# Small identity products into unread PSUM banks, at twelve places of TensorE's program

## What is computed

```python
for layer in range(2):
    shift, scale, gate = modulation(silu(c), w_mod[layer])      # c_ctx for context tokens
    h = x * (1 + scale) + shift
    if layer == 0:                                             # even
        q, k, v, g, gates = split(h @ w_in)
        y = concat(retention(q, k, v), mlstm(q, k, v, gates)) @ w_out
    else:                                                      # odd
        q, k, v = split(h @ w_in)
        y = concat(gqa(q, k, v), diff_attention(q, k, v)) @ w_out
    x = layer_norm(ALPHA * x + gate * y)
    x = layer_norm(ALPHA * x + gate2 * peer(modulate(x)))       # product keys, top 16, expert rows
```

## Time and profile before

| what | value |
|---|---|
| time, median of three executions | 2671.81 us (2669.43 to 2677.14) |
| the profiled execution's own time | 2669.78 us |
| its span, first to last instruction | 2668.0 us |
| mean granted clock of TensorE | 0.989 |
| PE busy | 2596.5 us (97%), 15833 matmul instructions |
| DVE, ACT, POOL busy | 1658.8 (62%), 1021.3 (38%), 721.4 us (27%) |

### The profile page before, as it was taken

The page is one execution under the profiler, slowest core; times in us unless marked ns, Lnnn a source line. Parts: engine busy times, 40 slices in busy tenths (PEclk is TensorE's granted clock), DMA queues, the critical chain, the costliest instruction groups (busy, mean ns, idle before and its releaser), DMA issues. The chain is left out here.

```text
span 2668.0 us, 39467 instructions
## 1 busy us (share of the span) xinstructions
PE 2596.5 (97%) x15833; PEld 2300.9 (86%) x15833; DVE 1658.8 (62%) x3309; ACT 1021.3 (38%) x1531; POOL 721.4 (27%) x688
## 2 busy tenths in 40 slices
PE   7998999999999999999999989999999999999998
PEld 6997799999999997777779679999999999777775
DVE  3447789888344455555576469987934445655556
ACT  3434433345333333333353553334533333333333
POOL 1001020000111136777712003000011112777773
PEclk9998999999999999999999899999999999999999
DMA  9653474457798869999964624344779886999995
GB/s 308 214 172 139 166 239 138 159 200 296 294 340 312 310 244 389 389 384 380 388 192 147 212 97 154 108 164 168 288 281 360 309 316 223 390 389 391 393 385 202
DMA packets 233941, 708.88 MB, mean 266 GB/s; under 512 B 22432, under 2 KB 154912, under 8 KB 211488
## 3 DMA queue, kind: packets, MB, share of 16 engines
q1 hardware_dynamic: 172912, 516.86, 53.1%
q0 software_dynamic: 60032, 189.01, 19.2%
q10 hardware_dynamic: 816, 0.48, 0.1%
HBM read 602.31 MB, written 103.98 MB: 265 GB/s over the span
## 5 line engine op out<-in xcount | busy, mean ns | idle before, releaser
L1411 PE MATMUL hidden_ps<-h_hi,u_hi 128*128 128x384 f32 x2016 | 680.2, 337 | 4.3 <-issue 3.3
L1411 PE MATMUL hidden_ps<-h_hi,u_lo 128*128 128x384 f32 x2016 | 673.9, 334 | 0.0
L1411 PE MATMUL hidden_ps<-h_lo,u_hi 128*128 128x384 f32 x2016 | 673.9, 334 | 0.0
L2301 DVE TENSOR_TENSOR v_lo<-v_slot,v_hi 128x1024 fp32r<-128x1024 f32 x248 | 303.8, 1225 | 273.1 <-ACT v_hi L2165 273.0
L2165 ACT ACTIVATE v_hi<-v_slot 128x1024 fp32r<-128x1024 f32 x248 | 263.0, 1060 | 514.7 <-PE out_ps L2094 513.0
L2094 PE MATMUL out_ps<-v_hi,act_hi 128*128 128x512 f32 x992 | 389.6, 393 | 0.0
L2094 PE MATMUL out_ps<-v_lo,act_hi 128*128 128x512 f32 x992 | 386.3, 389 | 0.0
L2094 PE MATMUL out_ps<-v_hi,act_lo 128*128 128x512 f32 x992 | 385.9, 389 | 0.0
L1411 PEld LDWEIGHTS hidden_ps<-h_hi,u_hi 128*128 128x128 f32 x2016 | 378.6, 188 | 7.0 <-issue 7.0
L1411 PEld LDWEIGHTS hidden_ps<-h_lo,u_hi 128*128 128x128 f32 x2016 | 378.7, 188 | 0.0
L1411 PEld LDWEIGHTS hidden_ps<-h_hi,u_lo 128*128 128x128 f32 x2016 | 378.5, 188 | 0.0
(11 more groups left out here) (510 smaller groups left out, 3956.1 us busy)
## 6 DMA issues: line engine op xcount, KB each, us to landing
u_slot<-in_peer_u SPq DMA_DIRECT2D x64, 2048.0 KB, 8.9
v_slot<-in_peer_v SPq DMA_DIRECT2D x64, 2048.0 KB, 10.2
hidden<-hidden_ring SPq DMA_DIRECT2D x64, 768.0 KB, 5.8
spread_gates<-spread SPq DMA_DIRECT2D x16, 2048.0 KB, 7.3
hidden_in<-hidden SPq DMA_DIRECT2D x64, 512.0 KB, 14.6
ada_w_ring<-in_ada_w SPq DMA_DIRECT2D x48, 512.0 KB, 5.0
even_w_ring<-in_even_w SPq DMA_DIRECT2D x16, 1024.0 KB, 7.5
ada_w_ring<-in_ada_w SPq DMA_DIRECT2D x16, 1024.0 KB, 6.1
```

Of the source, the lines that this page charges most:

```text
L1411: mm = pe.matmul(PH_[:, b, 0:T], u[:, b, k * P:(k + 1) * P], x[:, k, :], start=(k == 0 and part == 0), stop=(k == KB - 1 and part == 2))
L2301: dve.tensor_tensor(lo, V[o // JC % 2][:, o % JC, :], hi.bitcast(F32), ALU.subtract).then_inc(vl, 1)
```

## The change

The helper becomes `hold_clock(pe, bank, n)`, which issues n such products into the first 128 columns of a bank that is named at each call. It takes no semaphore and signals none. The two calls at the front grow from 6 to 18 and 26, and ten more calls are put in, with 4, 8, 12, 20, 16, 6, 16, 24, 24 and 24 products (in the order of the diff). Two waits are new: in `even_project` on `mix_taken`, and at the end of `odd_project` on `taken`; they make sure that the bank has been read by its real reader.

```diff
--- before.py
+++ after.py
@@ -144,6 +144,11 @@
                     mm = pe.matmul(PR[32 * i:32 * i + 2, m % 2, 0:HALF_COLS], CT[:, 4 * kk + i, :], AW[:, 4 * kk + i, :],
                                    start=(kk == 0), stop=(kk == 1))
             mm.then_inc(used, 1)
+
+        def hold_clock(pe, bank, n):
+
+            for _ in range(n):
+                pe.matmul(bank[:, 0:P], ident, ident, start=True, stop=True, skip_group_check=True)
 
         def cond_slot(k, q):
 
@@ -361,10 +366,6 @@
                             if g == PAIRS - 1:
                                 mm.then_inc(item_done, 1)
 
-                    def keep_warm(n):
-                        for _ in range(n):
-                            pe.matmul(PG[:, 0:P], ident, ident, start=True, stop=True)
-
                     def ret_begin(h):
                         if h:
                             pe.wait_ge(o_taken, h)
@@ -416,13 +417,13 @@
                     pe.transpose(PG[:, 0:2 * DEPTH * 2 * KB], LNR[:, :],
                                  CST[0:2 * DEPTH * 2 * KB, C_IDENT:C_IDENT + 2 * DEPTH * 2 * KB]).then_inc(ln_turned, 1)
                     pe.wait_ge(lnc_done, 1)
-                    keep_warm(6)
+                    hold_clock(pe, PG, 18)
                     pe.wait_ge(xt_taken, KB)
                     first_mod(0)
                     first_mod(1)
                     first_columns(0)
                     first_columns(1)
-                    keep_warm(6)
+                    hold_clock(pe, PG, 26)
                     for g in range(PAIRS):
                         if g + 1 < PAIRS:
                             first_mod(2 * g + 2)
@@ -485,8 +486,11 @@
                                 mm = pe.matmul(PG[:, 6 * R + i * 6:6 * R + (i + 1) * 6], CST[0:R, C_SEL + i * P:C_SEL + (i + 1) * P],
                                                SM[:, :, :].rearrange("p t j -> p (t j)"), start=True, stop=True)
                             mm.then_inc(small_done, 1)
+                    pe.wait_ge(mix_taken, TT)
+                    hold_clock(pe, PG, 4)
                     pe.wait_ge(row_ready, REST // 4)
                     part_columns(pe, PM, ROW, PICK, (REST // 4 - 1) % 2, N_MOD - 1, turned)
+                    hold_clock(pe, PG, 8)
 
                 @block.scalar
                 def _(act):
@@ -1069,6 +1073,7 @@
                         mm.then_inc((f_half, f_done)[n], 1)
                         if (t, n) == (0, 1):
                             turn_mix(2)
+                    hold_clock(pe, PT[:, 0], 12)
                     turn_tile(pe, PF, 1, normed, x_turned)
                     groups = front_groups(PQ, PH_, WQH, UH)
                     pe.wait_ge(first_w, 4)
@@ -1282,6 +1287,7 @@
                             if t == TT - 1 and k == 0:
                                 turn_tile(pe, PF, 0, normed, x_turned)
                         mm.then_inc(f_done, 1)
+                    hold_clock(pe, PT[:, 0], 20)
                     turn_tile(pe, PF, 1, normed, x_turned)
                     groups = front_groups(PQ, PH_, WQH, UH)
                     pe.wait_ge(first_w, 4)
@@ -2490,6 +2496,9 @@
                                     mm = pe.matmul(PJ[:, item % 4, 0:NW], h[:, k, t * P:(t + 1) * P], w[:, k, :],
                                                    start=(k == 0 and part == 0), stop=(k == KB - 1 and part == 2))
                             mm.then_inc(done, 1)
+                    items = NCH * TT - TAKEN
+                    pe.wait_ge(taken, items - 3)
+                    hold_clock(pe, PJ[:, items % 4], 16)
 
                 @block.scalar
                 def _(act):
@@ -2658,6 +2667,7 @@
                         for k, x in enumerate(src):
                             mm = pe.transpose(banks(n)[:, k * P:(k + 1) * P], x, ident)
                         mm.then_inc(turned, 1)
+                    hold_clock(pe, PO[:, 1], 6)
                     for taken in (turn_taken, turn_taken_v):
                         pe.wait_ge(taken, len(TURNS) // 2)
 
@@ -2720,6 +2730,8 @@
                     for n in range(len(GROUPS)):
                         if n + 1 < len(GROUPS):
                             scores(n + 1)
+                        if n == 0:
+                            hold_clock(pe, PO[:, 1], 16)
                         modulation(n)
                         pe.wait_ge(e_done, n + 1)
                         if n >= 1:
@@ -2731,6 +2743,7 @@
                         if n:
                             weighted(n - 1)
                     weighted(len(GROUPS) - 1)
+                    hold_clock(pe, PT[:, 0], 24)
 
                 @block.scalar
                 def _(act):
@@ -2952,6 +2965,8 @@
 
                     def states(h):
                         pe.wait_ge(k_rows, h + 1)
+                        if h == H - 1:
+                            hold_clock(pe, PK, 24)
                         for n, (t, d) in enumerate(KINDS):
                             if h and n % 2 == 0:
                                 pe.wait_ge(cu_taken if n else nc_taken, h)
```

## The result

The changed kernel takes 2681.76 us (median of 8 executions, 2681.05 to 2684.15), the kernel before beside it 2672.84 (8 executions, 2669.4 to 2677.14): ratio 1.0038, 95% interval 1.0028 to 1.0047. It is slower by 8.9 us, clear of noise and above the 8.0 us that the prediction took as the bound; forecast were 2685.2, +15.4 on the profiled run. The profiled execution of the changed kernel took 2681.65 us, with a span of 2679.9.

A forecast was written before the change was run, and what follows sets the result against it. The prediction took TensorE, busy 2596.5 of 2668.0 us, to bound the kernel. Its terms by place summed to +15.4 on the profiled 2669.8, giving 2685.2 us, with a range from 2670 to 2696.

The forecast's parts named there:

- The price: At every hold: one call, two instructions, costs 0.255 us, so 186 more calls add 47.4 us of PE work.
- rival 3: All holds: a long run of calls is cheaper than six, at 0.18 us a call; sum +0.9, 2671, no change; chance 0.10.
- Before the mLSTM: 4 and 8 calls at the joint: start +1.8 us later, 2.5 gained from the clock behind; −0.7.
- Last states: 24 calls in the mLSTM ahead of four products: DVE's copy goes from 241.02 to 245.1; +4.1 us.
- mLSTM's end: 24 calls at the mLSTM's end: +4.2 us of delay, 2.7 gained in the low stretch behind; +1.5.
- Even output block: 12 calls, 3.06 us, in a pause of 1.85; no low stretch behind, so nothing comes back; +1.2 us.
- Into attend: Calls of 16, 6 and 16: delays 3.6, 0.6 and 2.0 us, 4.7 back where exponentials set the pace; +1.5.
- Odd output block: 20 calls, 5.10 us, ahead of eight transpositions; the low stretch lies ahead of the hold; next_ht waits longer; +5.1 us.
- Front: 18 and 26 calls at the kernel's start: the better clock is gained and given away; +1.1 us.
- Rival 1: All holds: they don't keep the clock up, so the gains go; 26.5 us later, about 2696, slower; chance 0.09.
- rival 2: Delays are absorbed later, since what follows a block waits for HBM weights; sum 6.7, 2676, no change; chance 0.15.
- rival 4: All holds: loads of a repeated operand cost nothing, 0.12 us a call; sum −8.2, 2662, faster; chance 0.08.

The follow-up runs named there:

- e2: The changed kernel without the 24 calls ahead of the mLSTM's last states: 2677.17 us, ratio 1.0028 to the kernel before.
- e6: The kernel before with only the 16 calls in attend's first group added (the two new waits stay in): ratio 0.9993 to the kernel before.
- e1: The changed kernel without the 20 calls in the odd output block: 2677.76 us, ratio 1.0034 to the kernel before.
- e3: The changed kernel with the two calls at the front at 6 and 6 as in the kernel before: 2682.68 us, ratio 1.0049 to the kernel before.
- e11: The changed kernel with 40 calls for 20 in the odd output block: 2685.48 us, ratio 1.0046 to the kernel before.
- e12: The changed kernel itself, measured and profiled again without any edit: 2682.65 us, ratio 1.0038 to the kernel before.
- e10: The kernel before plus calls at last states (24), even output block (12), odd projection's end (16), odd output block (20) alone: 2683.14 us, ratio 1.0041.
- e7: The change with all counts cut to the pauses, and without the 4 and 8 calls in attend: ratio 0.9968 to the kernel before.
- e5: The changed kernel without calls at the last states, even output block, odd projection's end and odd output block: 2675.96 us, ratio 1.0011 to the kernel before.
- e9: The change with all counts cut to the pauses, and without the 6 calls in the even output block: 2665.74 us, ratio 0.9972 to the kernel before.

## Why the prediction was right, and where it was not

The side and the mechanism were right: the holds keep the clock up, their overhang costs more than they give, and it is handed on. The size was not: +15.4 worked out, +8.9 measured, within the range given. That 2681.76 lies only 3.4 from the 2685.2 is partly luck: the sum was laid on an execution of 2669.78, and the median of before beside the change is 2672.84. By its own steps:

- **The price.** 0.255 us was the row of six calls; runs of 18 to 40 cost 0.223 to 0.234. The prediction's own sums are +15.4 at 0.255 and +0.9 at 0.18, so about +10.6 at 0.23: the price makes some 4.8 of the 6.5 us that were too many. Six, 18, 26 and 40 calls took 1.53, 4.21, 5.98 and 8.93 us; by these a call is some 0.22 and a run some 0.2 more, once (an estimate), which weighs most on the row of six. It was rival 3 in part. The Trainium skill's pair ("TensorE: Matmul & The Clock Gate", Back-to-back issue gap), 81 ns, stays below the 0.1115 to 0.117 that an instruction took here.
- **Before the mLSTM**, −0.7: the joint cost 1.4 (4.67 − 3.24) for 1.8, and 3.1 came back for 2.5 (26.75 − 23.66 in e2). −1.7. That is against the draw of the clock in before; e6, without calls there, has a shorter stretch and 24.81, against which only 1.2 came back.
- **Last states**, +4.1: 3.5 in e1, e3, e11 and e12, and 5.0 in the first profile, where the hold ran partly at half clock (5.1 in e10). So of the seven stretches this one stayed, in part, and the last, which the prediction left low, was high. Against its block's start DVE's last copy was 1.9 and 0.4 later in the two profiles of the change, not 4, since the better clock ahead of it gave back; in e10, without the joint's calls, 5.1.
- **mLSTM's end**, +1.5: 3.2 of delay (4.2 forecast), 2.7 of gain as forecast (1.5 against e6 and e10, whose stretch there is shorter: 34.33). +0.5.
- **Even output block**, +1.2: 0.7 of delay. That nothing is behind it was wrong: it keeps out a stretch that costs 5.3 to 5.4 us where it falls. The step "no low stretch is behind it" read one execution as a rule.
- **Into attend**, +1.5: 2.9 and 1.9 of delay, against 3.6 and 2.6, and 4.6 of gain in the walk (4.7 forecast). +0.2. ACT did set the pace: PE waits on exp_t in the walk after.
- **End of attend**, +1.6: 2.0 of delay and 1.1 of gain. +0.9.
- **Odd output block**, +5.1: 4.4. That its stretch at 1587 would stay was wrong for both profiles of the change, e2 and e3, and right for e1, e7, e10 and e11. Against its block's start next_ht came 2.2 us later, not 5, since 1.1 came back at the start and that stretch was missing.
- **Front**, +1.1: −0.3 in the first profile; the weights were there when the shorter holds ended. The gate products start at 90.3 to 91.2 us in the six profiles with 18 and 26 calls, at 90.6 to 92.7 in the four with 6 and 6, so the front costs nothing.

The corrected terms, each against the profiles named: −0.3 − 1.7 + 3.5 + 0.5 + 0.3 + 0.2 + 0.9 + 4.4 = +7.8 (the even output block with the 0.34 that came back behind it), near the 8.9 of the medians. Of the first profile's 11.9, 3.1 are the stretch at 92 us and 1.5 the half clock in the last states' hold, and the one at 1587 is missing, −1.2.

Rival 1 is refuted by the windows, rival 2 by e10 and by the landmarks (1606.06 to 1617.79 and 11.9 at the end of the span; and from PEER's first row to DVE's last copy in the odd projection 1146.8 us before, 1147.1 in the change, which starts there 7.0 us later, and 1147.1 in e10, 5.8 later), rival 4 by the price.

## What the runs showed that was not expected

Executions of one kernel differ by which half-clock stretches they have, and this makes most of their spread. The 56 executions of the kernel before that ran beside the experiments have mean granted clocks of 0.987 to 0.991; those at 0.987 (11) average 2676.2 us, those at 0.990 (14) 2668.2: 2.7 us for 0.001, which is what half clock costs if PE sets the pace throughout (0.001 × 2670). The correlation is −0.90. The changed kernel's eight first executions lie within 3.1 us of each other and the eleven of e12 within 6.5, those of before within 7.7 and 12.3 beside them. Some of the stretches that come and go stand at short pauses (1.88 us idle between 326 and 334 us in e12; 1.85 ahead of the even output block's turn of tile 1 in e5, e6 and e9, where the clock falls 1 to 2 us behind the turn's start, and 1.68 behind this turn in e2), one behind 16 products of six columns (90.78 to 92.96 us in the changed kernel). Why the clock falls there in one execution and not in the next stays open; no run isolated it. Nor was it tried to move the last states' hold ahead of its wait, into the whole of its pause, as ACT still reads that bank.

## What to carry to other kernels

Put filler work only where it ends before the awaited event, at its price in a run of that length: the same idea lost 0.38% with generous counts and won 0.36% with counts cut to the pauses. Read a delay from landmark to landmark in several profiles, since one profile shows one draw of the clock. A place without a low stretch in one trace may still need the filler.
